# Activations in two planes 64 bytes apart modulo 128, and slabs of eight wide products and then eight narrow ones

## The reference, cut to what matters

```python
proj = h @ w_in                                      # hybrid layer
return jnp.concatenate([y_a, y_b], axis=-1) @ w_out
gate_b, gate_c, u, z = jnp.split(h @ w_in, 4, axis=-1)   # short convolution
return (y * jax.nn.silu(z)) @ w_out
```

## Time and profile before

| what | value |
|---|---|
| median of 3 runs | 3014.7 us (3014.14 to 3017.23) |
| profiled execution, its own time | 3016.94 us |
| span of the profiled execution | 3015.2 us |
| mean granted TensorE clock | 0.994 |
| TensorE matmul busy | 2949.6 us, 98% |
| TensorE weight load busy | 2567.2 us, 85% |
| VectorE busy | 2158.2 us, 72% |
| ScalarE busy | 1505.2 us, 50% |
| HBM traffic | 208 GB/s over the span |

### The profile page before, as it was taken

One profiled execution on the slowest core, in us unless ns is written; L12 is line 12 of the kernel. 1 busy time (PEld: TensorE's weight loads), 2 busy tenths in 40 slices (PEclk: granted clock), 3 DMA queues, 4 the chain that ended last, 5 costly groups with the idle time before them and its releaser, 6 DMA issues.

```text
span 3015.2 us, 51441 instructions
## 1 busy us (share of the span) xinstructions
PE 2949.6 (98%) x17510; PEld 2567.2 (85%) x17510; DVE 2158.2 (72%) x3030; ACT 1505.2 (50%) x2164; POOL 452.3 (15%) x187
## 2 busy tenths in 40 slices
PE   7999999999999999999999999999999999999998
PEld 6889999889988888888887877788887888888887
DVE  6666666766668888888887889876687436565466
ACT  4454444444444444444444777766544444444443
POOL 0111011110100000000000000000002445545443
PEclk9999999999999999999999999999999999999999
DMA  6443434444457887888875454456785566766655
GB/s 213 145 139 132 133 131 141 144 134 143 150 191 262 313 293 279 315 304 305 297 290 197 163 169 168 165 193 214 245 301 181 190 207 223 244 237 236 207 182 175
DMA packets 172691, 629.42 MB, mean 209 GB/s; under 512 B 19224, under 2 KB 20376, under 8 KB 171808
## 3 DMA queue, kind: packets, MB, share of 16 engines
q1 hardware_dynamic: 165024, 601.99, 57.1%
q10 hardware_dynamic: 7552, 25.91, 2.5%
HBM read 615.22 MB, written 12.60 MB: 208 GB/s over the span
## 4 chain that ended last, share of the span: by engine, by line
PE 68%; issue 25%; DVE 4%; ACT 2%; DMA 1%; DVEq 0%; SPq 0%; POOL 0%; ACTq 0%; POOLq 0%
PE gemm L537 41%; PE gemm L542 20%; PE side L678 1%; DVE wl L1528 1%; PE side L685 1%; ACT wh L984 1%; PE side L690 1%; DMA raw<-in_stream 1%; PE side L563 0%; DVE xs L1617 0%; DMA x<-in_x 0%; PE side L745 0%; DVE gB L1729 0%; ACT gA L1086 0%; PE side L722 0%
## 5 line engine op out<-in xcount | busy, mean ns | idle before, releaser
L537 PE MATMUL gemm<-xs,wh 128*128 128x512 f32 x5120 | 1646.0, 403 | 25.1 <-DVE stage L1533 7.3
L984 ACT ACTIVATE wh<-raw 128x1024 fp32r<-128x1024 f32 x939 | 984.2, 1057 | 925.3 <-PE gemm L542 806.2
L1528 DVE TENSOR_TENSOR wl<-raw,wh 128x1024 fp32r<-128x1024 f32 x811 | 1034.2, 1279 | 445.5 <-ACT wh L984 426.1
L542 PEld LDWEIGHTS gemm<-xs,wl 128*128 128x128 f32 x5120 | 965.3, 189 | 226.0
L542 PE MATMUL gemm<-xs,wl 128*128 128x256 f32 x5120 | 1011.8, 279 | 0.0
L537 PEld LDWEIGHTS gemm<-xs,wh 128*128 128x128 f32 x5120 | 783.2, 189 | 54.1 <-issue 47.0
L537 PE MATMUL gemm<-hid,wh 128*128 128x512 f32 x2368 | 747.6, 397 | 6.6 <-DVE fxg L1533 2.2
L542 PEld LDWEIGHTS gemm<-hid,wl 128*128 128x128 f32 x2368 | 446.9, 189 | 100.9
L542 PE MATMUL gemm<-hid,wl 128*128 128x256 f32 x2368 | 468.6, 279 | 0.0
L1457 POOL TENSOR_TENSOR wl<-raw,wh 128x1024 fp32r<-128x1024 f32 x128 | 349.0, 2732 | 368.5 <-ACT wh L984 368.5
L537 PEld LDWEIGHTS gemm<-hid,wh 128*128 128x128 f32 x2368 | 357.5, 188 | 9.4 <-ACT wh L984 3.2
(11 more groups left out here) (385 smaller groups left out, 1964.0 us busy)
## 6 DMA issues: line engine op xcount, KB each, us to landing
raw<-in_stream SPq DMA_DIRECT2D x940, 512.0 KB, 4.0
ada_a<-in_ada SPq DMA_DIRECT2D x144, 512.0 KB, 5.1
ada_b<-in_ada SPq DMA_DIRECT2D x48, 512.0 KB, 5.1
stash<-stage ACTq DMA_DIRECT2D x12, 512.0 KB, 3.6
att<-stash ACTq DMA_DIRECT2D x8, 384.0 KB, 4.3
x<-in_x SPq DMA_DIRECT2D x4, 512.0 KB, 5.6
xacc<-in_x ACTq DMA_DIRECT2D x1, 2048.0 KB, 11.6
stash<-stA ACTq DMA_DIRECT2D x4, 512.0 KB, 6.8
```

The costliest lines, as they stand in the source:

```text
L537: mm(G[n][:, :], wh[:, slot, at:at + P], rhs(sl * SLAB_K + k), start=sl == 0 and k == 0, stop=False, skip_group_check=True)
L542: op = mm(G[n][:, T:2 * T], wl[:, slot, at:at + P], rhs(sl * SLAB_K + k)[:, 0:T], start=False, stop=last, skip_group_check=True)
L984: A(wh[:, slot, :], raw[:, slot, :], ACT.Copy).then_inc(hi_ready, 1)
L1528: tt(wl[:, slot, :], raw[:, slot, :], wh[:, slot, :].bitcast(F32), ALU.subtract).then_inc(lo_ready[slot], 1)
```

## The change

Three things are changed.

1. *Layout.* `xs`, `hid` and each half of `hid2` become two planes, a low one and behind it a high one, with a gap of 16 words (64 bytes) between them. All low planes start at 0 modulo 128, and all high planes at 64 modulo 128 (`xs`: 65664 and 82112). A wide product reads 256 low columns and then 256 high ones from two places; a narrow product reads high columns, at 64 modulo 128. The PSUM halves change their roles with it. `hid` is moved to the same place modulo 512 as `xs`. The helpers `xs_part`, `hid_part` and `hid2_part` give ScalarE and VectorE the same elements as before.
2. *Order.* An inner slab runs its eight wide products, then calls the first hook, waits for `lo_ready`, runs its eight narrow products, counts up `slab_used` and calls the second hook. Edge slabs keep the order W W n n.
3. *Places of other tiles.* `toep`, `crs`, `t1`, `mSb`, `stA`, `fsum`, `yg` and others move to the room that the planes leave.

```diff
+GAP, LO, HI = 16, 0, 1
-    xs = place("xs", [P, KC, 2 * T], F32R)
+    xs = place("xs", [P, 2, KC * T + GAP], F32R)
+    top[0] += (xs_at - top[0]) % 512
     hid_at = top[0]
-    hid = place("hid", [P, 24, 2 * T], F32R)
+    hid = place("hid", [P, 2, 24 * T + GAP], F32R)
-    hid2 = nc.alloc_sbuf_tensor_at("hid2", [P, 32, 2 * T], F32R, offset=hid_at)
+    hid2 = nc.alloc_sbuf_tensor_at("hid2", [P, 2, 2, 16 * T + GAP], F32R, offset=hid_at)
...
+            def high(sl, slot, n, k):
+                at = (k * SLAB_N + n) * P
+                mm(G[n][:, :], wh[:, slot, at:at + P], rhs(sl * SLAB_K + k), start=sl == 0 and k == 0, stop=False,
+                   skip_group_check=True)
+
+            def low(sl, slot, n, k):
+                at = (k * SLAB_N + n) * P
+                return mm(G[n][:, T:2 * T], wl[:, slot, at:at + P], rhs(sl * SLAB_K + k)[:, HI, :], start=False,
+                          stop=sl == nslabs - 1 and k == SLAB_K - 1, skip_group_check=True)
+
             for sl in range(nslabs):
                 q, slot = q0 + sl // RING, sl % RING
                 wait(pe, hi_ready, 4 * q + slot + 1)
+                if 0 < sl < nslabs - 1:
+                    ready(sl)
+                    for n in range(SLAB_N):
+                        for k in range(SLAB_K):
+                            high(sl, slot, n, k)
+                    if hook is not None:
+                        hook(slot0 + 2 * sl)
+                    wait_lo(pe, q, slot)
+                    for n in range(SLAB_N):
+                        for k in range(SLAB_K):
+                            op = low(sl, slot, n, k)
+                    op.then_inc(slab_used, 1)
+                    if hook is not None:
+                        hook(slot0 + 2 * sl + 1)
+                    continue
                 wait_lo(pe, q, slot)
                 ready(sl)
...
         def xs_of(k):
-            return xs[:, k, :]
+            return xs[:, :, k * T:(k + 1) * T]
...
-            o, y = xs[:, 2 * s:2 * s + 2, 0:T], norm_y_buf[n][:, 2 * (s % 2):2 * (s % 2) + 2, :]
+            o, y = xs_part(HI, 2 * s, 2), norm_y_buf[n][:, 2 * (s % 2):2 * (s % 2) + 2, :]
```

More of the change, by code:

```diff
@@ L144, in program, with chunks_of, xs_part, hid_part @@
     xacc = nc.alloc_sbuf_tensor_at("xacc", [P, KC, T], F32, offset=xs_at)
+    def chunks_of(ap, n):
+        return ap.rearrange("p (n t) -> p n t", n=n)
+    def xs_part(part, k, n):
+        return chunks_of(xs[:, part, k * T:(k + n) * T], n)
+    def hid_part(part, k, n):
+        return chunks_of(hid[:, part, k * T:(k + n) * T] if isinstance(k, int) else hid[:, part, bass.ds(k * T, n * T)], n)
+    def hid2_part(part, k, n):
+        if isinstance(k, int):
+            return chunks_of(hid2[:, k // 16, part, k % 16 * T:(k % 16 + n) * T], n)
+        return chunks_of(hid2[:, 0, part, bass.ds(k * T, n * T)], n)
     def V(name, a=0, n=None):
@@ L535, in group @@
                     for k in range(SLAB_K):
-                        at = (k * SLAB_N + n) * P
-                        mm(G[n][:, :], wh[:, slot, at:at + P], rhs(sl * SLAB_K + k), start=sl == 0 and k == 0,
-                           stop=False, skip_group_check=True)
+                        high(sl, slot, n, k)
                     for k in range(SLAB_K):
[L540 to L543, removed]
+                        op = low(sl, slot, n, k)
                     if n == SLAB_N - 1:
@@ L779, in hid_of, with hid2_of @@
         def hid_of(chunks):
-            return lambda k: hid[:, chunks[k], :]
+            return lambda k: hid[:, :, chunks[k] * T:(chunks[k] + 1) * T]
+        def hid2_of(first):
+            return lambda k: hid2[:, (first + k) // 16, :, (first + k) % 16 * T:((first + k) % 16 + 1) * T]
         def outa_ready(sl):
@@ L808, in _ @@
         for i in range(4):
-            group(G_SCOUT + i, Q_SCOUT + 3 * i, 12, lambda k: hid[:, k, :], sc_ready,
+            group(G_SCOUT + i, Q_SCOUT + 3 * i, 12, hid_of(range(24)), sc_ready,
                   at_slot(21, lambda: earlier(2)) if i == 3 else None)
@@ L1131, in attn @@
                 act.wait_ge(S("yb"), it + 1)
[L1132 removed]
+                A(hid_part(HI, 16 + it, 1), yb[:, :].unsqueeze(1), ACT.Copy).then_inc(S("yb_hi"), 1)
         def heads(it):
@@ L1186, in sc_round @@
             act.wait_ge(S("sc_y"), j + 1)
-            A(hid[:, 4 * j:4 * j + 4, 0:T] if isinstance(j, int) else hid[:, bass.ds(4 * j, 4), 0:T],
+            A(hid_part(HI, 4 * j, 4),
               yv[:, :, :], ACT.Copy).then_inc(S("sc_hi"), 1)
@@ L1777, in delta @@
                 yv2 = yh[:, :, :].rearrange("p (v c) i -> p v (c i)", v=2)
-                low(hid[:, bass.ds(2 * it, 2), T:2 * T], yv2, hid[:, bass.ds(2 * it, 2), 0:T]
+                low(hid_part(LO, 2 * it, 2), yv2, hid_part(HI, 2 * it, 2)
                     ).then_inc(S("ya_lo"), 1)
@@ L1950, in sc_round @@
                     dve.wait_ge(S("sc_hi"), j + 1)
-                    o = hid[:, 4 * j:4 * j + 4, :] if isinstance(j, int) else hid[:, bass.ds(4 * j, 4), :]
-                    low(o[:, :, T:2 * T], yv[:, :, :], o[:, :, 0:T]
+                    low(hid_part(LO, 4 * j, 4), yv[:, :, :], hid_part(HI, 4 * j, 4)
                         ).then_inc(S("sc_lo"), 1)
```

68 lines of the change are left out of this document (35 added, 33 removed).

## The result

The changed kernel takes 3032.9 us (median of 4 runs, 3030.18 to 3035.28), the kernel before, beside it, 3014.8 (3014.14 to 3017.23): 1.0058 of it, 95% interval 1.0046 to 1.007. It is 18 us slower, where 16 us less were forecast. The profiled execution took 3030.8 us (span 3029.0) at a mean granted clock of 0.994. That is the clock of the profiled execution of before, so between these two traces, whose spans are 13.8 us apart (3015.2 and 3029.0), the clock explains nothing.

What follows compares the result with a forecast made beforehand. TensorE's products, 98% of the span, were taken as the bound. Gains of 13.6 us in inner slabs, 1.1 in edge slabs and 1 at hooks made 15.7 off 3014.7: 2999 us, range 2940 to 3036, the forecast's own 2985 to 3008.

Steps and rivals of the forecast that it cites:

- The bound: Whole kernel: TensorE's matmuls fill 98% of the span, so a nanosecond on a product is a nanosecond of the end.
- Wide in a run of eight, 0.230: Inner slabs: each wide product takes 0.230 us, from an earlier run of 16 wide products; bounds 0.217 and 0.2325.
- Narrow in a run, 0.1155: Inner slabs: each narrow product in a run of eight keeps its present mean of 0.1155 us; bounds 0.109 and 0.120.
- Edge slabs, 1.1 us won: Edge slabs, order kept: the 160 on `xs` gain 7 ns each from the narrow reads' new phase, 1.1 us.
- Hooks, bounds 3 gained to 5 lost: Inner slabs: first hook comes 0.46 us later, some stalls go, some chains tighten; 1 us gained, bounds 3 gained to 5 lost.
- The wait for the low weights, at nothing: Inner slabs: the wait moves behind eight wide products, bringing at most 0.6 us; its gain and its instruction costed at nothing.
- D: Rival, chance 0.25: inner slabs' narrow runs are bound by the weight load at 0.120 us a product; 25 us lost, 3040 us.
- B: Rival, chance 0.2: opposite phases remove most of the products' excess in inner and edge slabs; 2945 us.
- C: Rival, chance 0.2: no measurable change, within 0.2% or 6 us; wide products stay at 0.2325 us; 3011 us.

Runs made afterwards that it cites:

- rope_waits: The changed kernel with one more wait: GpSimd's last rotary product waits for VectorE's low split of slab 5 of the head; 3018.0 us, 1.0009 of before.
- bench: No network: TensorE alone runs 18 stretches of 128 products, in four orders with operands at different addresses; units W W n n with activations at 0 take 0.6966 us.
- bench2: TensorE alone again, 28 stretches of 128 products at more operand addresses; a unit takes 0.6913 us with weights at 0 and activations at 64, at most 0.7129.
- layout_alone: The changed kernel with its planes kept, but the old order W W n n in every slab; 3021.6 us, 1.0019 of before.
- hook_at_six: The changed kernel with the first hook called after six of the eight wide products; 3018.9 us, 1.001 of before.
- order_alone: The kernel before with its old layout, taking only the new order of the inner slabs; 3021.6 us, 1.0027 of before.

## Why the prediction was wrong

Two steps failed, and they are of like size. Forecast and result are 34 us apart (2999 and 3032.9). `rope_waits`, the change without its stall, is at 3018.0. So 19 of the 34 us are the forecast price of the products, where 15 us of gain were summed and none came. The other 15 lie between `rope_waits` and the changed kernel: the hooks, taken as 1 us of gain, with 2 to 4 us that go with the clock.

*The bound.* Right in the main: less time for a product is less at the end. Moving `xs` and `hid` gave 12 us, of 16 to 20 by the products.

*Wide in a run of eight, 0.230: wrong.* The row that I took the earlier trace rows was at the good place without my knowing: `xs` at 65664 and `wab2` at 124480 are 64 apart modulo 256, and `bench` has 0.2291 for it. I read it as the price of "opposite phase modulo 128", and gave half of it to the new read. Measured are 0.233 in the kernel and 0.2333 alone. The step named its own weak point (no row shows the jump from plane to plane, 5.5 us for each nanosecond) and then costed the jump at nothing. To a place 64 bytes apart it costs 6.5 ns in the long run, and 3.4 in runs of eight (0.2333 against 0.2299 for planes both at 0 in `bench2`).

*Narrow in a run, 0.1155: nearly right as a mean, wrong as a picture.* Runs are at 0.114 or at 0.118, a whole run at one of them. Over all runs of eight in the trace of after that nothing interrupts (491 narrow and 483 wide), the starts give 0.1164 and 0.2327. The inner slab so comes to 2.792 us on `xs` and 2.794 on `hid`. The two slabs of before in the earlier trace rows were typical: over all uninterrupted units of that trace they are 2.788 and 2.775. That makes 480 x 4.3 ns + 212 x 18.4 ns = 6 us lost in place of 13.6 won.

*Edge slabs, 1.1 us won: wrong in sign.* A unit in planes takes 0.6988 alone, against 0.6966 and 0.6938 of the old places, and over the edge slabs of after 0.6988 and 0.6998, against 0.6969 and 0.6938 before. That is 640 x 1.9 ns + 336 x 6 ns = 3 us lost. The sum has a gap that stays open. By its products `rope_waits` would be 9 us over before, and its medians say 3 (interval of its ratio up to 0.18%, or 5 us). `layout_alone`, where all 3744 units are in planes, would be 11.5 us over by `bench`, and measured 6.

*Hooks, bounds 3 gained to 5 lost: wrong by 10 us or more, and outside the bounds.* The 0.46 us were right, and so was the slack that I read the earlier trace rows, for VectorE's steps by themselves. What I left out is what stands between them. A hook that comes 0.46 us later delays not only its own chain but the high split that is queued behind ScalarE's hook work, then VectorE's low split, and this moved past a GpSimd instruction on the same port. I wrote that the split has 2 us to spare, which was true of TensorE's need for the slab. I did not ask what VectorE does *after* the split. That is `Em`, for which TensorE already waited up to 0.3 us, and I took these waits to go. They became seven of 1.3 us. The 3.31 us of GpSimd's last rotary addition stood in the trace of before, 0.9 us over what it takes alone, and was the sign that the two already touched.

*The wait for the low weights, at nothing: right.* No wait at the middle of a slab shows in the lists.

*The rivals.* D had the sign and came within 7 us (3040), and that is luck: it had no stall. It wanted 0.120 for all narrow products from the weight load; they are at 0.1164. Alone in a run they take 0.1199 at 0, 0.1178 at 64 and 0.1167 at 32 with the same loads, so it is at least not the load alone that sets them. B fell: the excess over 0.640 is there in `bench` with all other engines at rest, and at the best place is still 51 ns (0.6913). C, no change within 0.2%, describes `rope_waits` (1.0009), that is, the change without the stall. The last sentence of the prediction, that a wide read may pay for its jump, turned out true, but it is only part of a small loss.

*Ledger of the 18 us:* some 11 for the stall (10 to 11 in the traces by the end of the heads; 14.9 and 14.0 by the medians of `rope_waits` and `hook_at_six`, from which 2 to 4 go with the clock), and about 3 for the products, by an interval that reaches down to zero. Together they are the 13.8 us between the two traces at one clock. The other 4 of the 18 us show only between the medians, at clocks of 0.9935 and 0.995; by the estimate above some 2 of them go with the clock, and the rest is not explained.

## What to carry to other kernels

A hook that moves by half a microsecond moves everything queued behind it on every engine. Follow that to the first place where VectorE and GpSimd start within a microsecond of each other and one of them takes longer than it does elsewhere. Ask who comes first afterwards; a wait on the engine that has time puts it right. And before a layout is built on a rule of addresses, run the bare instruction at eight or so offsets of both operands: here it would have shown in 20 us of TensorE's time each that the rule had the wrong period, and that shifts of two buffers by 64 and 128 bytes were worth 12 us, with the order kept and no planes.

## What was not expected of the hardware

- The rate of full-rate products depends on the difference between the address of the activations and that of the weights, with everything else at rest: units of 0.6913 to 0.7129 us over all stretches. It depends on the place of `wh` against `wl` as well. All places tried fit a period of 256 bytes. Why is open, and so are the 51 ns that the best place still takes over 0.640.
- A wide read in two pieces is free if they are at the same place modulo 256 (0.2268 for 0.2269 in one piece), and costs 6.5 ns in a long run if they are 64 apart (0.2333).
- In one kernel and with one layout a run of eight narrow products goes at 0.114 or 0.118, and stays there for the run. Both occur on `xs` (95 of 308 uninterrupted runs at the lower) and on `hid` (59 of 183), which lie at the same place modulo 512. Both occur in `bench` too, in one stretch with no other engine at work (activations at 64), while with the change's planes all runs there are at 0.113. What selects it is open.
- In `order_alone` the same addition took 2375 ns in one head and 3486 in another, because two engines started within about 0.2 us of each other. A small change can decide such a race otherwise, which is the likely reason why two parts at 6 to 8 us each made 18.
